# Reordering the six matmuls of a dense slice over the two PSUM banks of its tile

## What is computed

```
h = rmsnorm(x)
P = h @ w_in                              # 1024 -> RWKV, sparse attention, retention, gates
y_rw, y_sa, y_ret = the three mixers, each from its columns of P
merged = gate0 * (y_rw @ w_br_rwkv) + gate1 * (y_sa @ w_br_dsa) + gate2 * (y_ret @ w_br_ret)
x = x + merged @ w_o
x = x + square(relu(rmsnorm(x) @ w_up)) @ w_down      # width 4096
```

## Time and profile before

| | |
|---|---|
| median of 3 runs | 2961.14 us |
| lowest, highest | 2960.81, 2964.19 us |
| the profiled execution | 2957.23 us |
| its span, first to last instruction | 2955.4 us |
| mean granted TensorE clock | 0.943 of full |

### The profile page before, as it was taken

One profiled execution on the slowest core, in us unless ns is written; L12 is line 12 of the kernel. 1 busy time (PEld: TensorE's weight loads), 2 busy tenths in 40 slices (PEclk: granted clock), 3 DMA queues, 4 the chain that ended last, 5 costly groups with the idle time before them and its releaser, 6 DMA issues.

```text
span 2955.4 us, 61291 instructions
## 1 busy us (share of the span) xinstructions
PE 2691.1 (91%) x24862; PEld 2460.6 (83%) x24862; DVE 1309.7 (44%) x2092; ACT 575.8 (19%) x1233; POOL 1032.4 (35%) x596
## 2 busy tenths in 40 slices
PE   7978899599998999999989789995999989999997
PEld 6877688389887989999988678874998789899997
DVE  3245885433337442332252468844343363522332
ACT  2112223411212120110111112233121211200111
POOL 3502232011223545555533033320222245455553
PEclk9979899699999999999999799986999999999999
DMA  4201112111133312222232111111111343222221
GB/s 169 87 28 62 42 58 71 57 46 48 51 120 116 122 59 85 85 79 84 85 106 73 36 58 47 61 64 46 58 51 54 120 135 98 65 86 79 84 85 53
DMA packets 64552, 222.53 MB, mean 75 GB/s; under 512 B 7888, under 2 KB 8656, under 8 KB 63056
## 3 DMA queue, kind: packets, MB, share of 16 engines
q1 hardware_dynamic: 43200, 158.23, 16.8%
q10 hardware_dynamic: 21136, 61.17, 5.9%
HBM read 190.34 MB, written 29.03 MB: 74 GB/s over the span
## 4 chain that ended last, share of the span: by engine, by line
PE 79%; DVE 10%; DVEq 5%; issue 3%; ACT 2%; ACTq 1%; DMA 0%
PE dense L460 62%; PE mix L460 15%; DVEq L1348 5%; ACT region_b L934 1%; DVE region_b L1528 1%; DVE region_b L1582 1%; PE mix L837 1%; DVE region_b L1584 1%; DVE region_a L1367 1%; DVE in_lo L1701 0%; DVE region_b L1641 0%; DVE region_b L1595 0%; DVE x L1563 0%; PE mix L535 0%; DMA x<-in_x 0%
## 5 line engine op out<-in xcount | busy, mean ns | idle before, releaser
L460 PE MATMUL dense<-act_hi,w_hi 128*128 128x288 f32 x3296 | 969.8, 309 | 40.0 <-DVE act_lo L1360 29.0
L444 POOL TENSOR_SCALAR w_hi<-w_raw 128x1024 fp32r<-128x1024 f32 x296 | 312.5, 1056 | 1865.6 <-PE dense L460 1502.8
L460 PE MATMUL dense<-act_lo,w_hi 128*128 128x288 f32 x3296 | 929.7, 297 | 0.0
L447 POOL TENSOR_TENSOR w_lo<-w_raw,w_hi 128x1024 fp32r<-128x1024 f32 x296 | 719.8, 2432 | 24.7
L460 PEld LDWEIGHTS dense<-act_hi,w_hi 128*128 128x128 f32 x3296 | 626.9, 190 | 103.8 <-issue 49.2
L460 PE MATMUL dense<-act_hi,w_lo 128*128 128x288 f32 x3296 | 707.3, 296 | 0.0
L460 PEld LDWEIGHTS dense<-act_lo,w_hi 128*128 128x128 f32 x3296 | 628.4, 191 | 0.0
L460 PEld LDWEIGHTS dense<-act_hi,w_lo 128*128 128x128 f32 x3296 | 534.5, 190 | 0.0
L460 PE MATMUL dense<-in_hi,w_hi 128*128 128x288 f32 x1408 | 399.0, 297 | 23.9 <-DVE y_mix L1710 12.6
L460 PE MATMUL dense<-in_lo,w_hi 128*128 128x288 f32 x1408 | 398.4, 298 | 0.0
L460 PE MATMUL dense<-in_hi,w_lo 128*128 128x288 f32 x1408 | 304.8, 298 | 0.0
(11 more groups left out here) (180 smaller groups left out, 2583.5 us busy)
## 6 DMA issues: line engine op xcount, KB each, us to landing
w_raw<-in_stream SPq DMA_DIRECT2D x296, 512.0 KB, 3.5
y_mix<-gate_scratch ACTq DMA_DIRECT2D x48, 288.0 KB, 2.8
gate_scratch<-region_b ACTq DMA_DIRECT2D x36, 288.0 KB, 2.1
x_scratch<-x ACTq DMA_DIRECT2D x2, 2304.0 KB, 8.9
y_scratch<-y_mix ACTq DMA_DIRECT2D x2, 2304.0 KB, 8.0
x<-x_scratch ACTq DMA_DIRECT2D x2, 2304.0 KB, 10.0
y_mix<-y_scratch ACTq DMA_DIRECT2D x2, 2304.0 KB, 9.5
gate_scratch<-region_a ACTq DMA_DIRECT2D x12, 288.0 KB, 2.1
```

Source lines behind the costliest of these rows:

```text
L444: nc.gpsimd.tensor_scalar(w_hi[:, v, :], w_raw[:, s, :], 1.0, 1.0, ALU.mult, ALU.mult).then_inc(w_high, 1)
L447: nc.gpsimd.tensor_tensor(w_lo[:, v, :], w_raw[:, s, :], w_hi[:, v, :].bitcast(F32), ALU.subtract).then_inc(w_split, 1)
L460: return nc.tensor.matmul(out, lhsT, rhs, start=start, stop=stop, skip_group_check=True)
```

## The change

In `dense_slice`, the two matmuls with `w_hi` that were issued together for one half of the tokens (hi, then lo) now stand in two loops over the halves. The order of a slice by operand and half was hi/0, lo/0, hi/1, lo/1, then w_lo with hi/0, hi/1; it becomes hi/0, hi/1, lo/0, lo/1, then w_lo with hi/0, hi/1. Half 0 lies in the first bank of the buffer and half 1 in the second. Nothing else is changed.

```diff
                 parts = [(slice(512 * i, 512 * i + HALF), slice(HALF * i, HALF * i + HALF)) for i in range(2)]
                 for out, tok in parts:
                     acc(buf[:, out], wh, hi[:, x_k, tok], first, False)
+                for out, tok in parts:
                     acc(buf[:, out], wh, lo[:, x_k, tok], False, False)
                 for out, tok in parts:
                     mm = acc(buf[:, out], wl, hi[:, x_k, tok], False, stop)
```

## The result

The changed kernel takes 2968.37 us (median of 12 runs, 2963.11 to 2971.22) against 2959.41 us for the kernel before (12 runs, 2952.52 to 2964.19). The ratio is 1.003, 95% interval 1.0021 to 1.0038: 9 us slower, more than the 0.2% that the prediction took as the least that can be told. That is outside its band for no difference (2956 to 2967 us, 2961 the centre) and inside its whole range (2941 to 2980 us). The profiled executions differ by 13 us (spans 2968.4 and 2955.4 us); a few us of that are the scatter of single runs.

What follows compares the result with a forecast made beforehand. The prediction took TensorE's dense matmuls to bound the kernel. Its terms, 0 (counts) + 0 (waits) + 0 (reads) + 0 (bank), laid on the median of 2961.1 us, gave 2961.0 us, range 2941 to 2980 us.

Steps and rivals of the forecast that it cites:

- band for no difference: Whole kernel: a time of 2956 to 2967 us, not told apart from no change; chance 0.44.
- What bounds the kernel: Dense matmuls of line 460, 62% of the span: nearly every nanosecond added to or taken from one lands in the time.
- Counts, waits and signals: In each slice: matmuls and weight loads stay the same, no wait or signal moves; cost 0.
- The bank order: In each slice, two of six steps turn from same-bank to other-bank, 4704 in all; taken as 0.
- The bound of 38 us: Loss if all 4704 changed steps cost 8 ns more; upper bound for the bank order.
- the w_lo row of the slow stretch: At 2431 us, 138.1 ns a matmul: w_lo has 306 ns against 298 for lo.
- What TensorE reads: In each slice: same pairs of stream and weight load, only the halves streamed second and third exchanged; cost 0.
- the bar of 2.5 ns a slice: Least difference a measurement can tell from no change: some 0.2% of the time, 5.9 us.
- A price for the bank change: Rival, first-to-second and third-to-fourth matmul steps: 2 ns each, 9.4 us slower, 2970.5 us; chance 0.25.
- The shorter rhythm: Rival, dense matmuls: strict bank turns settle steps at 130.2 ns; 26 us less, or 2948 us with half; chance 0.28.
- The clock: Rival, TensorE: short idle times from bank turns drop the granted clock; 10 us of work takes 18, 2969 us; chance 3%.
- the handing over of the loaded weights: Full-clock matmul steps: example source of the 10 to 14 ns above the columns' 120 ns; its number and order stay.

Runs made afterwards that it cites:

- the first experiment: Against the kernel before: operands in the old order, but sent to the banks 0 1 0 1 0 1, mixing the halves; 2956.57 us, ratio 1.000.

## Why the prediction was wrong

**What bounds the kernel** held: a dense matmul's step lands in the time. By the chain's pieces it rose from 132.1 and 132.6 ns to 133.4 ns in the MLP; the pieces listed above add up to 9.8 us, and the time rose by 9 us.

**Counts, waits and signals**, each costed at 0, held: the counts are those of the earlier trace rows, no new wait stands among the longest, and the run with the old streams and the banks in turn has the same work behind the same waits and the time of before.

**The bank order**, the one term that wasn't thought plainly zero, was rightly taken as 0. The term asks for a bank that changes while the streams stay, and the first experiment is just that. With 4704 more changes of bank the ratio is 1.000 (0.9991 to 1.0008), and with one bank a slice nothing is gained. The bound of 38 us above it came from the w_lo row of the slow stretch, which was read as the mark of a change of bank. It may as well have been its place in a rhythm: the changed kernel's timeline shows the longer step wander over all products.

**What TensorE reads** is the step that failed. It said that the pairs of a stream and the load beside it are the same set as before. "Only which half is streamed third and second is exchanged. Cost: 0 as far as the rows show." The runs put the loss there: the halves in turn cost it with either order of tensors and under three arrangements of the banks (ratios 1.003 to 1.0042), the order of before is free of it with either order of tensors (1.000 and 1.0001), and moving the second start by 128 bytes makes the two orders alike. The size that the term should have had is 9 us, 3.8 ns a slice. The rows did hold a warning: one order, with the same instructions, took 130 to 134 ns a step, and 138 once. The prediction saw that such a spread is wider than the bar of 2.5 ns a slice and even said so, but gave the unexplained spread no term, only rivals that named other causes.

**The rivals.** A price for the bank change gave 2970.5 us, the right side and nearly the right number, for a cause that the runs exclude; that is luck. The shorter rhythm came out the other way round: strict turns of the banks alone left the retention pieces at 43.75 us, and strict turns of the halves put every long piece at the long value. The clock didn't fall: the mean granted clock is 0.943 in both kernels. The case that the Trainium skill tells of (TensorE: Matmul & The Clock Gate, A second HAM failure mode: psum-queue depth-cycling) didn't arise here. The prediction also held against this kernel a figure of the Trainium skill for the gap (TensorE: Matmul & The Clock Gate, Back-to-back issue gap), columns / 2.4 + 2.5 ns. The Trainium skill states it there for a single matmul by itself, and says that in a stream of weight loads and matmuls both set the spacing. The trace has such a stream, and its surplus is not 2.5 ns: 256 columns are 106.7 ns at 2.4 GHz and the step is 119 ns by the estimate above. The measurement decides. That the surplus comes from the handing over of the loaded weights, which the prediction offers as an example, no run shows.

**The tests that the prediction set itself** worked. It said it would be wrong if the long MLP pieces moved by over 2 us each in one direction, "for then the order of banks or of halves sets the rhythm"; they moved by 3.9 and 2.3 us. The 2.3 us alone would have been weak, being no more than the order of before varies by itself; both layers moving to one value, and the retention pieces with them, is what carries it.

**What stays open.** Why the start of a stream matters. Shown is that, in the orders tried, starts of 0 and 1024 bytes act alike, and 128 and 1152; that 64 acts differently from both in the MLP; and that the effect depends on the sequence of starts and on the stage. Whether the reads from SBUF or the weight loads beside them are the place of it was not measured. Open too is why the order of before has MLP pieces of 400.1 us in one layer and 402.6 us in the other, with the same instructions. A layout whose rows put both halves on a start of 256 bytes was only imitated (1.001 and 1.0016), not built, and these ratios promise nothing over the kernel before.

## What to carry to other kernels

Where matmuls run back to back and bound the kernel, the order in which pieces of the moving operand are streamed, and where in memory they start, can move each step by 1% (2.5% in the retention pieces here, 43.75 to 44.85 us) although no instruction, wait or operand changes. Read the step from the chain's long pieces (length over count) before such an edit: if the same code shows several values, a reordering may not be free, and its sign can't be argued from counts. And when an edit is named for one effect (banks in turn), cross it with the other thing that it changes before believing the name.

## What was not expected of the hardware

- The order of the PSUM banks had no effect that can be told: with the streams of the changed kernel, one, four or six changes of bank a slice gave MLP pieces of 404.95, 404.97 and 404.94 us.
- A start moved by 128 bytes changed the MLP piece by 2.3 us of 405 (404.94 to 402.62), and made two orders equal to 0.01 us in the pieces.
- With the halves in turn the steps repeat every four matmuls, three of 131 ns and one of 140 ns, across slices of six.
- Swapping the last two matmuls of each slice, which have the same weights and tensor, cost 0.41%.
- The step follows the columns at 256 and at 288, with 10 to 14 ns on top of the columns' own time (an estimated 119 ns at 256, 130 to 134 ns at 288), while weight loads run beside it.
